# Rows that TensorE streams: from 1040 bytes apart to 1024 bytes apart, at chosen addresses

## What is computed

```python
def first_block(...):                       # DEPTH = 2
    for i in range(DEPTH):
        h = h + 0.5 * swiglu(rmsnorm(h, ffn1_norm[i]), ffn1_w_gu[i], ffn1_w_down[i])
        u = rmsnorm(h, mix_norm[i])
        b_g, c_g, v_c, q_c, kv_c, k_r, g_conv, g_mla = jnp.split(u @ w_in[i], split_pts, axis=-1)
        y_conv = short_conv_branch(b_g, c_g, v_c, conv_w[i], w_conv_out[i])
        y_mla = mla_branch(q_c, kv_c, k_r, ...)
        merged = sigmoid(g_conv) * y_conv + sigmoid(g_mla) * y_mla
        h = h + merged @ w_o[i]
        h = h + 0.5 * swiglu(rmsnorm(h, ffn2_norm[i]), ffn2_w_gu[i], ffn2_w_down[i])
        gate = sigmoid(rmsnorm(h, ple_norm[i]) @ w_ple_gate[i])
        h = h + gate * (p[i] @ w_ple_proj[i])
    return rmsnorm(h, final_norm)

def second_block(...):
    for i in range(DEPTH):
        u = rmsnorm_2(h, norm_mix_pre[i]) @ w_in[i]
        # sparse attention (top 64 keys by an index), a 31-tap convolution, pooling
        h = h + rmsnorm_2(mix @ w_out[i], norm_mix_post[i])
        m = square(relu(rmsnorm_2(h, norm_mlp_pre[i]) @ w_up[i])) @ w_down[i]
        h = h + rmsnorm_2(m, norm_mlp_post[i])
        h = h + sigmoid(h @ ple_gate[i]) * (p[i] @ ple_proj[i])
```

## The kernel before, in words

| buffer | before | after the change |
|---|---|---|
| x, rows 0 to 7 | 128/0, 144/16, 160/32, 176/48, 192/64, 208/80, 224/96, 240/112 | all 240/112 |
| inner tile, slot 0 | 128/192, 144/208 | all 176/48 |
| inner tile, slot 1 | 160/224, 176/240 | all 176/48 |
| gate, rows 0 to 7 | as x | all 192/192 |
| `mh`/`ml`, all rows | 128/128 | 128/128 |

## Time and profile before

### The profile page before, as it was taken

The page is one execution under the profiler, slowest core; times in us unless marked ns, Lnnn a source line. Parts: engine busy times, 40 slices in busy tenths (PEclk is TensorE's granted clock), DMA queues, the critical chain, the costliest instruction groups (busy, mean ns, idle before and its releaser), DMA issues.

```text
span 1978.2 us, 36952 instructions
## 1 busy us (share of the span) xinstructions
PE 1935.2 (98%) x16060; PEld 1916.9 (97%) x16060; DVE 1350.9 (68%) x1608; ACT 996.9 (50%) x1233; POOL 237.4 (12%) x168
## 2 busy tenths in 40 slices
PE   8999999999999999999999999998999999899999
PEld 8999999999999999999999999898999999799998
DVE  6655777775559655687785557896855589676556
ACT  5443545563437444545554445776533466654443
POOL 3000100010002000100010001473100016710000
PEclk9999999999999999999999999999999999899999
DMA  8555454465554655544556554424555543237551
GB/s 278 199 180 182 144 174 160 133 211 192 192 183 156 213 182 183 183 137 143 171 171 213 185 181 152 158 67 132 170 187 187 166 152 113 70 112 231 191 183 53
DMA packets 246533, 329.57 MB, mean 167 GB/s; under 512 B 6246, under 2 KB 218788, under 8 KB 246372
## 3 DMA queue, kind: packets, MB, share of 16 engines
q1 hardware_dynamic: 246018, 326.79, 50.0%
q0 software_dynamic: 96, 0.26, 0.1%
q10 hardware_dynamic: 258, 0.16, 0.0%
HBM read 326.14 MB, written 1.05 MB: 165 GB/s over the span
## 4 chain that ended last, share of the span: by engine, by line
PE 79%; DVE 12%; POOL 3%; ACT 3%; DMA 1%; issue 1%; SPq 0%; POOLq 0%; DVEq 0%; ACTq 0%
PE work L2028 17%; PE work L2029 17%; PE work L2030 17%; PE acc L2028 9%; PE acc L2030 9%; PE acc L2029 9%; DVE w_lo L1313 4%; POOL fa L747 2%; ACT w_hi L800 1%; DVE ra L1326 1%; DMA raw<-in_w_in_dram 1%; DVE xl L1347 1%; DVE fa L1358 1%; POOL fa L741 1%; PE acc L2105 1%
## 5 line engine op out<-in xcount | busy, mean ns | idle before, releaser
L1313 DVE TENSOR_TENSOR w_lo<-raw,w_hi 128x2048 fp32r<-128x2048 f32 (+2 forms) x313 | 709.8, 2271 | 107.8 <-ACT w_hi L800 105.8
L2028 PE MATMUL work<-xh,w_hi 128*128 128x256 f32 x2560 | 721.8, 282 | 9.6 <-DVE w_lo L1313 6.1
L2029 PE MATMUL work<-xl,w_hi 128*128 128x256 f32 x2560 | 718.6, 281 | 0.0
L2030 PE MATMUL work<-xh,w_lo 128*128 128x256 f32 x2560 | 717.0, 280 | 0.0
L800 ACT ACTIVATE w_hi<-raw 128x2048 fp32r<-128x2048 f32 (+2 forms) x313 | 576.6, 1849 | 165.4 <-PE work L2030 74.6
L2028 PEld LDWEIGHTS work<-xh,w_hi 128*128 128x128 f32 x2560 | 482.3, 188 | 13.9 <-issue 8.0
L2029 PEld LDWEIGHTS work<-xl,w_hi 128*128 128x128 f32 x2560 | 483.0, 189 | 0.3
L2030 PEld LDWEIGHTS work<-xh,w_lo 128*128 128x128 f32 x2560 | 483.1, 189 | 0.0
L2028 PE MATMUL acc<-ra,w_hi 128*128 128x256 f32 x1352 | 380.1, 281 | 0.0
L2030 PE MATMUL acc<-ra,w_lo 128*128 128x256 f32 x1352 | 379.7, 281 | 0.0
L2029 PE MATMUL acc<-ra,w_hi 128*128 128x256 f32 x1352 | 378.9, 280 | 0.0
(11 more groups left out here) (302 smaller groups left out, 2324.7 us busy)
## 6 DMA issues: line engine op xcount, KB each, us to landing
raw<-in_ffn_w_gu_dram SPq DMA_DIRECT2D x88, 1024.0 KB, 5.1
raw<-in_w_in_dram SPq DMA_DIRECT2D x52, 1024.0 KB, 5.5
raw<-in_ffn_w_down_dram SPq DMA_DIRECT2D x44, 1024.0 KB, 4.9
raw<-in_w_up_dram SPq DMA_DIRECT2D x32, 1024.0 KB, 5.3
raw<-in_w_down_dram SPq DMA_DIRECT2D x32, 1024.0 KB, 4.9
raw<-in_w_mla_out_dram SPq DMA_DIRECT2D x8, 1024.0 KB, 5.5
raw<-in_w_o_dram SPq DMA_DIRECT2D x8, 1024.0 KB, 4.9
raw<-in_w_ple_gate_dram SPq DMA_DIRECT2D x8, 1024.0 KB, 5.0
```

The lines of the kernel that those rows point to most:

```text
L1313: v.tensor_tensor(w_lo[:, s, 0:n], raw[:, r, 0:n], w_hi[:, s, 0:n].bitcast(F32), ALU.subtract).then_inc(lo_done.sem, 1)
L2028: pe.matmul(dst, ah, bh, start=start and i == 0, stop=False, skip_group_check=not group)
L2029: pe.matmul(dst, ah, bl, start=False, stop=False, skip_group_check=not group)
L2030: last = pe.matmul(dst, al, bh, start=False, stop=stop and i == len(pairs) - 1, skip_group_check=not group)
```

## The change

It gives x one buffer, and each of the three pairs rows exactly 256 elements (1024 bytes) apart, beginning at written-out places. No instruction is added, taken away or reordered; 12512 matmuls, 194 instructions of ACT and 198 of DVE get other addresses.

```diff
-ROW = T + 4
+X_SIZE, X_ROW, X_AT = 4160, 256, (28, 2108)
+H_ROW, H_AT = 256, (12, 1068)
+G_ROW, G_AT = 256, (4176, 6224)
...
-        xh = sb("xh", [P, KD, ROW], F32R)[:, :, 0:T]
-        xl = sb("xl", [P, KD, ROW], F32R)[:, :, 0:T]
+        x_rows = sb("x_rows", [P, X_SIZE], F32R)
...
+        def rows_at(arena, at, n, row):
+
+            return cut(arena, at, n, row)[:, :, 0:T]
+
+        xh, xl = (rows_at(x_rows, at, KD, X_ROW) for at in X_AT)
...
-        hh, hl = (cut(ra, i * 4 * ROW, 2, 2, ROW)[:, :, :, 0:T] for i in range(2))
+        hh, hl = (rows_at(ra, at, 4, H_ROW).rearrange("p (a b) t -> p a b t", a=2) for at in H_AT)
...
-        gh, gl = (cut(ra, 4 * ROW * 4 + i * KD * ROW, KD, ROW)[:, :, 0:T] for i in range(2))
+        gh, gl = (rows_at(ra, at, KD, G_ROW) for at in G_AT)
```

## The result

The changed kernel takes 1994.20 us (median of 4 runs, 1992.17 to 1995.18), the kernel before 1979.68 (4 runs, 1977.69 to 1982.07): ratio 1.0073, 95% interval 1.0061 to 1.0085. It is slower by 14.5 us. The forecast was 1973.2 us in a range of 1961 to 1990; both are wrong. The profiled execution spans 1992.2 us, 14.0 more than before, at a mean granted clock of 0.993 (0.994).

What follows compares the result with a forecast made beforehand. The prediction took TensorE's start-to-start matmul distance as the bound. Terms of -4.8 (x), -3.6 (inner tile) and +1.9 (gate) summed to -6.5 us, from 1979.7 to 1973.2 us, range 1961 to 1990 for 8 in 10.

Steps and rivals of the forecast that it cites:

- What bounds the kernel: TensorE, busy 98% of the span: the start-to-start distance of matmuls sets the end, a saved nanosecond counting 16,060 times at most.
- The address matters, by a few ns: Equal matmuls streaming from different addresses took 117.5 to 120.0 ns in the trace before, so a row's address moves the price.
- x at 240/112: Streamed x rows, high/low starts modulo 256: 116.9 ns instead of 117.5 over 8064 matmuls, 4.8 us saved.
- rival C: Hardly any difference: x costs 117.8 ns as it does standing in `pair`, total +0.7, 1980.4 us; chance 0.19.
- Above: 120.0 ns: Upper bound for the price of x, taken from `merged` at 128/128; at that price 20.2 us lost.
- Inner tile at 176/48: Accumulates of the inner tile: 117.2 ns instead of 118.2 over 3648 matmuls, 3.6 us saved.
- Gate at 192/192: Gate rows, 768 matmuls, priced at 120.0 ns like 128/128, 2.5 ns dearer: 1.9 us lost.
- x as stationary operand: Rows of x loaded as weights in block 2: costed at nothing, with 1.7 us either way.
- other engines, clock, waits: VectorE and ScalarE busy times, granted clock and waits of PE should stay; gain lost into waits under 1 us.
- D: Rival: a standing address is the dear case, x and inner tile up to 120.0 ns, 2008.4 us, half 1994; chance 0.28.
- the same in every unit: Sign in the profile after: each `project` unit of x should last 5.61 us instead of 5.64.

Runs made afterwards that it cites:

- three_240: The changed kernel with all three pairs (x, inner tile, gate) at 240/240: 1935.91 us, ratio 0.9783 to the kernel before.
- x alone: Against the changed kernel, inner tile and gate go back to rows 1040 bytes apart, only x stays moved (240/112): 1983.66 us, ratio 1.0022 to the kernel before.
- inner tile and gate alone: Against the changed kernel, x goes back to rows 1040 bytes apart, inner tile and gate stay moved: 1977.62 us, ratio 0.9986 to the kernel before.
- 16 entries: Matmuls-only kernel, 16 units per address pair, each behind three shorter matmuls of 16 to 256 columns: 240/112 ran at 122.2 ns in 3, 117.8 in 13.

## Why the prediction was wrong

- **What bounds the kernel**: right. Changes of the price came through to the end: 47.3 us by the distances of x, inner tile and gate in three_240, 43.7 in the time.
- **"The address matters, by a few ns"**: right, and the page of the Trainium skill on two independent ports did not decide here. That the pitch is no matter of its own was assumed and held.
- **x at 240/112, the step that failed.** I took 116.9 ns, "with two parts of 117.8 (it really stands) and one of 115.0", and summed 4.8 us saved. Measured: 120.0 in the mean, 17.5 us lost. Two things are wrong in it. The 115.0 of the earlier trace rows was no price of the pair: it was three matmuls on their way from one address to the next. The same bytes took 115.2 ns on average in that place before, 120.4 in the changed kernel and 118.1 in x alone, and no standing unit of x came under 117.6 in the changed kernel. And the 117.8 of the earlier trace rows, which was right to 0.1 ns for the fast rhythm, was nine matmuls of one entry; it could not show that the pair has a second rhythm at 122.2. With 117.8 alone the sum would have been rival C, 1980.4, still 14 us short; x alone came to 1983.7.
- **The sum itself.** I priced each buffer by itself and added. x alone costs 4 us, inner tile and gate alone gain 2.8, both together cost 14.5. The terms do not add, since the rows of one buffer have a say in the rhythm of the next buffer's: the same x rows at 240/112 had 63 slow units with the inner tile at 176/48 and 9 with the old one. The bound "Above: 120.0 ns" also broke: single units cost 122.2.
- **Inner tile at 176/48**: 117.2 was taken, 117.7 measured. 2.1 us gained and not 3.6, and 2.0 with x on its old rows. The tile kept its price in either company; what it did was to its neighbour.
- **Gate at 192/192**: 120.0 was taken from "the other pair with equal high and low address". Measured 117.8 and, in two whole units, 113.3, so 0.3 us gained and not 1.9 lost. That high and low are equal says nothing: 240/240 is at 113.3, 128/128 at 120.0.
- **x as stationary operand, other engines, clock, waits**: unchanged, as predicted. That was so for this change; at 240/240 the stationary rows cost 2.0 us more.
- **The rivals.** D had the sign: slower, from an x price over 118.0, and "half of it 1994 us" is what came. Its reason was not the right one. A standing address is not the dear case as such: at 192/192 the whole is back at the time of before, at 240/240 x alone brings 39 us against the changed kernel. I looked for units of one length, "the same in every unit", and for D for 5.70 us or more; in fact 63 units took 5.84 to 5.87 us and nearly all others 5.65 to 5.67. I gave it 0.28, and drew the range to 1990 through the middle of it.

## What to carry to other kernels

Where TensorE is the bound, the addresses of the streamed rows relative to the weights are a setting worth choosing: it made 3% between the changed kernel and three_240 (1994.2 and 1935.9 us). Read the start-to-start distance of whole units per buffer, and try pairs in a kernel of matmuls only, in the real sequence, for what stands ahead of a pair has a say in its price. Prefer one pair with a single rhythm for all buffers, over the pair that looks good by itself; a second rhythm can stay hidden, as that of 192/192 did in 16 entries. Do not price an address from three or nine matmuls between others, and do not add prices of neighbours that follow each other without a gap.

## What the runs showed of the hardware

- Dense groups of matmuls (high, low, high; 128 x 128 weights by 256 fp32r columns, full clock) settle in exact repeating patterns. Their means lie mostly (170 of 256 pairs) on a few steps: 113.3, 115.6, 116.7, 117.8, 118.9, 120.0. The changed kernel's units take the same times, to 0.1 ns per matmul, with ACT 50% and DVE 68% busy and the DMA traffic beside them, and without any of it.
- Some address pairs keep two patterns (240/112: 117.8 and 122.2; 176/48: 115.5 and 117.8; 64/64 and 192/192: 113.3 and 117.8). For the first two the run with 16 entries shows that the matmuls ahead pick between them.
- The price depends on the difference of the rows' and the weights' starts: after a common shift by 32 bytes it is the same within 0.2 ns in 244 of 254 comparisons. It does not depend on whether rows lie 1024 or 1280 bytes apart, in the two combinations tried. The lowest settled price of a unit in all these kernels is 113.3 ns.
